# Hybrid encoder trunk on one core: the table copy issued by SyncE, expert places in half points, ScalarE scaling and copying the probabilities

## What is computed

```
h  = rmsnorm(x);  z = h @ w_in                       # 5888 columns: q,k,v of A; q,k,v,gate of B; two gates
oa = softmax(q k^T/8 - slope*dist, sink) @ v         # mixer A: 8 heads, own chunk and two before, sinks
ob = norm(retention(q, k, v)) * silu(gate)           # mixer B: 4 heads, state carried from chunk to chunk
x  = x + (sigmoid(gA)*(oa@wa) + sigmoid(gB)*(ob@wb)) @ w_out
h2 = rmsnorm(x);  s = (h2 @ w_q) against two sets of 128 keys
idx, gate = top 16 of 16x16 sums, for each of 8 heads         # 128 experts a token out of 16384
y  = x + sum_k gate_k * gelu(h2 . U[idx_k]) * V[idx_k];  out = rmsnorm(y)
```

## Time and profile before

| | |
|---|---|
| median of three runs | 4188.11 us (4188.02 to 4191.79) |
| the profiled execution | 4192.38 us, span 4190.6 us |
| PE / DVE / ACT / POOL busy over the span | 79% / 59% / 25% / 43% |
| stage around the change: loop, tail | 1169 to 1742 us, 1742 to 1847 us |
| one interval of the loop (gate product L421 to the next) | 81.5 to 84.7 us, six of them |
| moved in one interval (1409 to 1492 us) | 25.66 MB, mean 309 GB/s |
| a copy's issue on POOL (L145, L146) | 0.51 to 0.72 us |
| last copies issued before and in the third interval | 1409.07 us, then 1447.21 us |
| last copy of all issued | 1711.7 us |
| PSUM copies L700 / L703 on DVE | 1.22 / 0.69 us |
| gate biases L422, operand copies L681 to L683, value copy L679, decayed keys L677 | 2.28, 1.48, 0.22, 0.87 us |
| three dots L1450 one behind the other | 3.4 us |
| block 1's last value used in the tail | 1773.5 us |

### The profile page before, as it was taken

How to read it: one execution, slowest core, us unless ns; L and a number is a source line. 1 busy time by engine, 2 the same in 40 slices (tenths; PEclk the granted TensorE clock), 3 DMA queues, 4 the chain that set the end, 5 groups by cost and what they waited for, 6 DMA issues and landing times.

```text
span 4190.6 us, 32116 instructions
## 1 busy us (share of the span) xinstructions
PE 3301.8 (79%) x8957; PEld 1648.5 (39%) x8957; DVE 2487.3 (59%) x5001; ACT 1049.8 (25%) x2852; POOL 1817.5 (43%) x1668
## 2 busy tenths in 40 slices
PE   8776599999737676848878878878977977977776
PEld 5453256666424444423323333323433423422222
DVE  0122168988856676564775674684585585486444
ACT  2101011111112222212333333333333333323322
POOL 1020137787823443203444444444444444445554
PEclk9877799999958787979999999999999999999999
DMA  9888979999986888729999999999999999999998
GB/s 344 310 285 301 321 251 413 411 409 412 413 342 260 322 324 312 276 120 412 421 418 421 421 409 408 422 419 401 422 414 408 422 414 409 422 414 420 422 422 354
DMA packets 303583, 1563.02 MB, mean 373 GB/s; under 512 B 31280, under 2 KB 59184, under 8 KB 179888
## 3 DMA queue, kind: packets, MB, share of 16 engines
q0 software_dynamic: 239616, 1342.28, 80.2%
q1 hardware_dynamic: 49216, 197.92, 12.0%
q10 hardware_dynamic: 14592, 21.10, 1.3%
HBM read 1517.54 MB, written 179.04 MB: 405 GB/s over the span
## 4 chain that ended last, share of the span: by engine, by line
DMA 25%; PE 18%; issue 6%; DVE 4%; ACT 1%; POOL 1%; POOLq 0%; ACTq 0%; DVEq 0%
DMA ring<-uv_d,IXD_p 25%; PE ps L1778 15%; PE ps L1750 3%; DVE ring L1877 2%; ACT dg L1821 1%; POOL ring L1981 1%; DVE CA_p L967 0%; PE ps L1767 0%; DVE BV_p L957 0%; ACT GE_p L1815 0%; DVE II_p L1315 0%; DVE SC_p L1320 0%; DVE CA_p L1375 0%; DVE DOT_p L1877 0%; DVE ACC L1858 0%
## 5 line engine op out<-in xcount | busy, mean ns | idle before, releaser
L1778 PE MATMUL ps<-ring,dg 128*128 128x512 f32 x3584 | 1700.3, 613 | 477.2 <-ACT dg L1821 453.4
L1981 POOL DMA_INDIRECT ring<-uv_d,IXD_p x896 | 1071.7, 1196 | 1326.3 <-PE ps L1778 1077.3
L1877 DVE CUSTOM_DVE_ANT_0 ring<-ring,H 128x1024 f32<-128x1024 f32 x896 | 1094.0, 1223 | 906.4 <-DMA ring<-uv_d,IXD_p 885.5
L1778 PEld LDWEIGHTS ps<-ring,dg 128*128 128x128 f32 x3584 | 660.9, 193 | 1434.5 <-ACT dg L1821 721.9
L1216 PE MATMUL ps<-w,xg 128*128 128x368 f32 x1792 | 556.0, 473 | 2.0 <-ACT SC_s L914 2.0
L1815 ACT ACTIVATE GE_p<-DOT_p 128x2 f32<-128x2 f32 x448 | 91.1, 203 | 1494.9 <-DVE DOT_p L1877 1494.9
L1216 PEld LDWEIGHTS ps<-w,xg 128*128 128x128 f32 x1792 | 341.3, 191 | 216.3 <-ACT SC_s L914 2.2
L1821 ACT ACTIVATE dg<-gdi,GE_p 128x128 f32<-128x128 f32 x896 | 310.8, 394 | 48.9 <-ACT GE_p L1815 4.7
L1809 ACT ACTIVATE gdi<-ident,GD_p 128x128 f32<-128x128 f32 x896 | 303.2, 386 | 28.4 <-issue 21.4
L145 POOL DMA_DIRECT2D uv_d<-in_peer_u x128 | 68.4, 534 | 490.6 <-DMA uv_d<-in_peer_v 258.6
L1485 POOL DMA_INDIRECT rv<-in_peer_v,IXD x80 | 94.9, 1187 | 271.5 <-DVE AC L1467 252.2
(11 more groups left out here) (417 smaller groups left out, 2935.0 us busy)
## 6 DMA issues: line engine op xcount, KB each, us to landing
uv_d<-in_peer_u POOLq DMA_DIRECT2D x128, 512.0 KB, 6.5
uv_d<-in_peer_v POOLq DMA_DIRECT2D x128, 512.0 KB, 8.1
w<-in_w_in SPq DMA_DIRECT2D x8, 2944.0 KB, 15.3
w<-in_w_in SPq DMA_DIRECT2D x16, 1472.0 KB, 9.4
z_d<-zo ACTq DMA_DIRECT2D x16, 1288.0 KB, 18.6
ring<-uv_d,IXD_p POOLq DMA_INDIRECT x896, 11.2
gates_p<-z_d SPq DMA_DIRECT2D x7, 1536.0 KB, 10.0
wq_s<-in_peer_w_q SPq DMA_DIRECT2D x8, 1024.0 KB, 13.7
```

The source lines that it names most:

```text
L1778: mm = T.matmul(bank(6 + n), dg[:, k % DR, :], ring[:, k % RS, D + n * 512:D + (n + 1) * 512], start=(k == 0), stop=(k == NK - 1))
L1877: V.tensor_tensor_reduce(out=row, in0=row, in1=H2[:], scale=1.0, scalar=0.0, op0=ALU.mult, op1=ALU.add, accum_out=DOT[:, k:k + 1]).then_in ...
L1981: g.indirect_dma_start(ring[:, n % RS, :], None, uv_d, bass.IndirectOffsetOnAxis(ap=IXD[:, n:n + 1], axis=0)).then_inc(s_ring[n % RS], 16)
```

## The change

Four things change, all in the mixers' blocks; the last stage only waits for one semaphore more.

1. SP issues the last 46 parts of the copy (`rest_of_table`), on its own queue: in blocks 3 to 7 three behind the key load, two behind the gate load and three behind the load of `x`; in block 8 two and four, so that the last four precede the tail's query weights. POOL issues none in this stage.
2. The points are cut into half points (V, then D): V0, D0, V1 before the merge, D1, V2, D2 behind it, V3, D3 after the norm, where V0, D0, V1, D1 stood before the merge, V2, D2 behind it and V3, D3 after the norm.
3. ScalarE scales the probabilities, one copy with a scale for each of the eight heads, before the sigmoids; it also copies both halves of the transposed probabilities and the attention output out of PSUM. This holds for blocks 1 to 8; block 0 keeps DVE's scaling.
4. In `dve_block` the query, decayed query and key copies come first, then the gate product, the value copy and the decayed keys, and last the gate biases (`dve_biases`). Increments of semaphores that nobody waits for are dropped.

```diff
+        s_uvs = sem("uv_table_rest")
+        def rest_of_table(sp, lo, hi):
+            for part in range(lo, min(hi, NEXP // P)):
+                sp.dma_start(uv_d[part * P:(part + 1) * P, 0:D], rows(t["peer_u"], part)).then_inc(s_uvs, 16)
+                sp.dma_start(uv_d[part * P:(part + 1) * P, D:], rows(t["peer_v"], part)).then_inc(s_uvs, 16)
...
-            def dve_probs(v, blk, width):
+            def dve_probs(v, blk, width, scaled):
...
-                V.tensor_tensor(pr, pr, rs[:].unsqueeze(2).to_broadcast([P, HA, width]), ALU.mult).then_inc(s["prob"], 1)
+                if scaled:
+                    V.tensor_tensor(pr, pr, rs[:].unsqueeze(2).to_broadcast([P, HA, width]), ALU.mult).then_inc(s["prob"], 1)
...
             act_exps(act, blk, 2 * P)
+            act.wait_ge(s["rden"], blk + 1)
+            for h in range(HA):
+                e = S.activation(Pr[:, h], Pr[:, h], ACT.Copy, scale=rs[:, h:h + 1])
+            e.then_inc(s["prob"], 1)
             if merge:
                 act_sigmoids(act, blk - 1)
             act.wait_ge(s["pt"], blk + 1)
-            S.activation(PT[:, 0:4].rearrange("p h c n -> p (h c n)"), bank(0, 2), ACT.Copy).then_inc(s["ptc"], 1)
+            for g in range(2):
+                S.activation(PT[:, 4 * g:4 * g + 4].rearrange("p h c n -> p (h c n)"), bank(2 * g, 2), ACT.Copy).then_inc(s["ptc"], 1)
             if merge:
                 act_mix(act, blk - 1)
+            act.wait_ge(s["oat"], blk + 1)
+            S.activation(oaT[:].rearrange("p j n -> p (j n)"), bank(0), ACT.Copy).then_inc(s["oatc"], 1)
             act_deviation(act, blk)
...
+            v.wait_ge(s["t1"], blk + 1)
+            V.tensor_copy(qbT[:].rearrange("p h n -> p (h n)"), bank(1))
+            if blk <= 2:
+                v.wait_ge(s_tab, 32 * blk)
+            V.tensor_tensor(qdT[:].rearrange("p h n -> p (h n)"), bank(1), into[:].rearrange("p h n -> p (h n)"), ALU.mult)
+            V.tensor_copy(kaT[:, 1], ps[:, 3, 0:P]).then_inc(s["qkv"], 1)
+            if merge:
+                dve_gate(v, blk - 1)
+            wait_mixers(v, blk, half)
+            step.did(V.tensor_copy(va[:, 1], z(VA, P, half)))
+            for h in range(HB):
+                q = V.tensor_scalar(kdec[:, h, :], z(KB + h * DK, DK, half), outd[:, h:h + 1], None, ALU.mult)
+            q.then_inc(s["kdec"], 1)
             if merge:
                 if blk == 3:
                     v.wait_ge(s_bw, 16 * 8)
-                dve_gate(v, blk - 1)
-            wait_mixers(v, blk, half)
...
+                dve_biases(v, blk - 1)
...
-            dve_point(v, blk, 0)
-            dve_point(v, blk, 1)
+            for half_point in range(3):
+                dve_point(v, blk, half_point)
             if merge:
                 dve_merge(v, blk - 1)
-            v.wait_ge(s["pt"], blk + 1)
-            V.tensor_copy(PT[:, 4:8].rearrange("p h c n -> p (h c n)"), bank(2, 2)).then_inc(s["ptc"], 1)
-            dve_point(v, blk, 2)
+            for half_point in range(3, 6):
+                dve_point(v, blk, half_point)
             v.wait_ge(s["oat"], blk + 1)
-            V.tensor_copy(oaT[:].rearrange("p j n -> p (j n)"), bank(0)).then_inc(s["oatc"], 1)
-
             V.tensor_copy(kaT[:, 0], kaT[:, 1])
...
             dve_retention_norm(v, blk, 2, step)
-            dve_point(v, blk, 3)
+            for half_point in range(6, 8):
+                dve_point(v, blk, half_point)
...
             def dve_point(v, blk, j):
-                grp = PTS * (blk - 2) + j
-                if blk > 2:
+                grp = PTS * (blk - 2) + j // 2
+                if j % 2:
+                    dve_expert_dots(v, grp)
+                elif blk > 2:
                     dve_expert_values(v, grp - PTS)
-                dve_expert_dots(v, grp)
...
                             load_keys_part(sp, blk + 1)
+                        part = TABLE_S + 8 * (blk - 3)
+                        if 2 < blk < NB - 1:
+                            rest_of_table(sp, part, part + 3)
+                            part += 3
...
                                 load_chunk(sp, 2)
+                            rest_of_table(sp, part, part + 2)
                             sp.wait_ge(s["x1"], blk)
...
                             load_rows(sp, blk)
+                            rest_of_table(sp, part + 2, part + 5 if blk < NB - 1 else NEXP // P)
...
                             pool_dots(g, grp)
-                            if blk > 2:
-                                part = TABLE_S + 2 * (grp - PTS)
-                                pool_table(g, part, min(part + 2, NEXP // P))
```

More of the change, by code:

```diff
@@ L228, in _ @@
                             mm.then_inc(s_mm, 1)
[L231 to L233 removed]
+        names = ("z1 z1b zq z2 xld t1 qkv scores sm_s sm_m sm_mx sm_d exp den rden prob pt ptc oat "
+                 "oatc st atm ro kvp stn stats var rs rstd yn silu ysil yt ytc ga gates ya "
+                 "mixb mix mixt mixtc wo x1 ssq2 ms2 sq2 r2 h2 x1st h2st kdec").split()
         s = {n: sem("b_" + n) for n in names}
@@ L593, in _ @@
                     dve_gate(v, 0)
+                    dve_biases(v, 0)
                     for h in range(HB):
@@ L845, in _ @@
                     dve_gate(v, 1)
+                    dve_biases(v, 1)
                     dve_merge(v, 1)
```

35 lines of the change are left out of this document (13 added, 22 removed).

## The result

The changed kernel takes 4165.88 us (median of four runs, 4164.1 to 4168.3), the kernel before 4189.64 (4188.02 to 4191.79) beside it: ratio 0.9943, 95% interval 0.9926 to 0.9961. The gain is 24 us, where 52 were forecast. The time lies in the range, at its upper end, and beside the 4165 of rival (2). The profiled execution took 4166.64 us around a span of 4164.8, against a span of 4190.6 before: -25.8.

What follows compares the result with a forecast made beforehand. No engine was full; DVE's chain, including gather waits, bound the loop, with PE 2.4 us behind. Six intervals gave -54, block 2 -2, block 1 +1, tail +3: -52, so 4136 us, range 4106 to 4168.

Steps and rivals of the forecast that it cites:

- rival (2): Loop: DMA engines are shared, so the gather wait moves rather than goes; interval 77 to 80, total 4165; chance 0.20.
- the term put at 2.2 for gate load and parts beside D2's rows: Mid-interval: 3.6 MB of gate load and two copy parts delay the rows by 2.2 us, between nothing and 5.
- the 71.8 with clear gathers: Loop interval in us between gate products if gate load and copy parts do not delay the rows; 74.0 was taken.
- The upper end, 5: Mid-interval: 5 us to pay if the gathers take the 10 to 12 us of landings behind table copies.
- They end at about +22 and fill the hole: Interval's start: SP's early copy parts, some 8 MB at 422 GB/s, take 20 us and fill the stretch without DMA.
- The tail: After the loop: four copy parts, 4.2 MB or 10 us, ahead of the query weights cost +3 us, between 0 and +10.
- Half of the queries' delay hides behind the expert tail: Tail: half the delay from four parts ahead of the query weights is covered by expert work ending at 1774.
- The last stage: Some 2330 us of gathers from the copied table: not touched by the change, so 0 us.
- Ahead of block 2: Start to block 2's gate product: -1 us, from block 2 at -2 and block 1 at +1.
- Two signs: Loop: DVE's gather waits under 6 us a block; second to fourth sets of rows landing under 8 us.
- the 78 that was to refute the forecast: Loop: an interval staying above 78 us would mean the long landings are the engines' own queue, not the copy's place.
- rival (1): Loop: gate load does not disturb the rows, interval 69.7 to 71.8, total 4116, perhaps faster PE scores; chance 0.20.

Runs made afterwards that it cites:

- later runs with the same loop: Changed kernel with the middle parts and last four issued behind the last values, once plain, twice with 24 DVE memsets: loops 444.0, 439.8 and 444.2 us.
- run with 16 late parts: Changed kernel with the 12 middle parts and last four issued in the tail, after DVE hands over the last expert sum: median 4137.8 us, ratio 0.9870.

## Why the prediction was wrong

Offsets from the gate product of the third interval, forecast / measured:

| step | forecast | measured |
|---|---|---|
| scores | +8.95 | +8.87 |
| reciprocal | +19.2 | +18.9 |
| ScalarE's scaling | 3.4 us | 3.31 |
| PT copies | +36.4 to +38.5 | +36.3 to +38.3 |
| last early part lands | +22 | +30.7 |
| V1's end | +34.7 | +35.5 |
| merge's end | +38.2 | +39.1 |
| PE's output product ends | +62.9 | +62.5 |
| D1, V2 end | +41.6, +45.9 | +42.5, +46.5 |
| D2 ends | +52.7 | +58.7 |
| residual | +65 | +70.7 |
| next gate product | 71.8, taken 74.0 | 77.5, mean 76.3 |

- **The step that failed in the loop** is the term put at 2.2 for gate load and parts beside D2's rows: "I take 2.2, nearer to the first, because they no longer stand behind the copy but beside it". Against the 71.8 with clear gathers the interval measured 5.7 more here and 4.5 in the mean (76.1 to 77.5 in five intervals, 72.3 in the last). Standing beside the copy did not help D2's rows: they landed in 9.2 to 11.3 us, and D2 ends 6.0 late, 5.4 of it its own. The upper end, 5 by the landings behind copies of the earlier trace rows, was the right row, and SP's issue order shows it: the parts follow the gate load at once, both ahead of the rows. Six times 2.3 is the 13.6 us by which the loop missed. Taking the parts out gave back 3.3 an interval, 2.2 to 3.0 in the later runs with the same loop.
- **A smaller step beside it** is "They end at about +22 and fill the hole; V1's rows are asked for at +24". The last early part was issued at 1404.01 and landed 17.9 us later, at +30.7. The forecast took the 422 GB/s of a stretch that holds mostly other loads; copies alone moved 317 (run with 16 late parts). In the first and the last interval, which have three early parts and not six, V1 ends at +34.8 and +34.5, near the forecast; in the other four at +35.2 to +35.7. Without the parts in the middle this is over half of what is left in the third interval: D2 ends 2.4 us late there, and 1.4 of them stand at V2's end already.
- **The tail** was put at +3 of 0 to +10, and measured +12.1. Two numbers failed in it: the delay itself ("4.2 MB or 10 us") and "Half of the queries' delay hides behind the expert tail". The query products ended 17.8 us later than before (+47.5 for +29.6), since each of the three weights behind the parts landed 19 to 20 us after its issue, for 9 to 10 before; and only the 6.2 us in which the queries had stood ready for ScalarE could hide.
- **The last stage** was said to be untouched, "the long last stage ... is not touched". Its code was not; the place of its loop in DVE's program was, and that cost 7.9.
- **Ahead of block 2** -1 was forecast and -5.4 measured; equal code spreads more than that, so it decides nothing.
- **Rival (2)** has the total and the mechanism of D2 (it gave D2's end as +58, D3 at +70.5, interval 77 to 80). It was right for D2's rows, not for D3's (landing 4.7 to 5.7 us), and for the total by chance: its loop was 13 us too poor, its tail 7 too good and the last stage's 8 not in it. Its 0.20 was too low: it rested on landings measured behind copies, my reading on a hope about the queue.
- **Two signs did not come**: DVE's waits for rows under 6 us a block (12.5) and landings of the second to fourth sets under 8 us (9.2 to 12.8 for D2's and V3's rows). The interval itself stayed below the 78 that was to refute the forecast.
- **The rest held**: DMA share 0.92, the hole filled, ScalarE's work hidden, PE 8 us ahead of the residual. PE's scores did not get faster, as rival (1) thought possible: 5.65 us again, at a granted clock of 0.50, the lower level of 1.2 GHz (third line of the first view), after PE had been idle for 13.70 us ahead of the transposes before them. The 3-3-2 order, which the working used as it stands, was not asked for its own worth in it; the run shows none while the rows are late.

## What to carry to other kernels

A bulk copy costs by what is asked for between its issue and its landing, on any queue, and here it lands up to 20 us after its issue where several stand together. So work out the landing from the rate that such copies show alone, and look for a stretch in which no load is awaited (here the search in the tail, some 60 us) and put the copy there, behind a wait that marks that stretch's start, rather than spread it among gathers; a place that only follows one of the waiting loads moves the collision to the next. And when instructions are added or removed ahead of a hot loop, compare the loop's stalls marked "issue" in both traces before crediting or blaming the change.

## What the runs showed of the hardware that was not expected

- A loop on DVE has a stall of 4.9 to 5.6 us at each round's start in every kernel here, and 24 instructions fewer ahead of it added a second of 2.3 to 2.7 us behind its second dot product. 24 dummy instructions ahead of it removed that. The runs show that the place in the program decides; by what means was not tried.
- DMAs issued by SP and by POOL delay each other as if they stood in one queue: rows that POOL asked for beside 3.6 MB of SP's landed in 9.2 to 11.3 us, beside the gate load alone in 6.8 to 7.2, with nothing ahead in 4.4 to 5.4.
- With nothing but the table's copy under way (1730 to 1770 us of the run with 16 late parts) the engines moved 317 GB/s at a DMA share of 1.03, where the stretch of the earlier trace rows had 422 at the same share.
